# A two-block transformer in float32 on one core: logarithm tables loaded behind the last gate function, embedding products kept in PSUM, and the output projections in another order

## What is computed

```python
# first block, layers i = 0 and 1
        x = x + mixer(rms_norm(x))
        x = x + conv_ffn(rms_norm(x, ffn_norm[i]))
        gate = jax.nn.sigmoid(rms_norm(x, ple_norm[i]) @ ple_w_gate[i])
        x = x + gate * (p[i] @ ple_w_proj[i])

# second block, layers i = 0 and 1
        x = x + mixer(rms_norm(x))
        h = rms_norm(x)
        x = x + (silu(h @ w1) * (h @ w3)) @ w2
```

## Time and profile before

| | us |
|---|---|
| median of the runs | 1351.99 |
| lowest and highest of 3 | 1349.96, 1353.1 |
| profiled execution | 1347.64 |
| its span, first to last instruction | 1345.9 |
| TensorE busy in it | 1303.2 (97%) |
| GpSimd, ScalarE, VectorE busy | 1011.1, 677.4, 652.5 |
| share of the chain of waits on TensorE | 82% |

### The profile page before, as it was taken

The page is one execution under the profiler, slowest core; times in us unless marked ns, Lnnn a source line. Parts: engine busy times, 40 slices in busy tenths (PEclk is TensorE's granted clock), DMA queues, the critical chain, the costliest instruction groups (busy, mean ns, idle before and its releaser), DMA issues.

```text
span 1345.9 us, 27777 instructions
## 1 busy us (share of the span) xinstructions
PE 1303.2 (97%) x11032; PEld 1254.4 (93%) x11032; DVE 652.5 (48%) x1160; ACT 677.4 (50%) x934; POOL 1011.1 (75%) x793
## 2 busy tenths in 40 slices
PE   7989999999989999999999999999999999999999
PEld 6879999999989888999999878999999898999999
DVE  8994465555565748555566474211113545311112
ACT  7715544444666756444346565444435445533442
POOL 1226898888777649888878794988887665988885
PEclk9999999999999999999999999999999999999999
DMA  6313675555535335555554532555554432555530
GB/s 265 127 64 127 183 248 181 176 179 183 188 128 182 103 124 171 185 185 187 185 175 143 188 134 95 197 178 182 185 187 165 139 114 93 188 189 188 180 131 31
DMA packets 33879, 217.07 MB, mean 161 GB/s; under 512 B 3683, under 2 KB 7428, under 8 KB 8196
## 3 DMA queue, kind: packets, MB, share of 16 engines
q1 hardware_dynamic: 30096, 211.14, 44.5%
q10 hardware_dynamic: 3700, 4.75, 1.4%
HBM read 213.26 MB, written 2.62 MB: 160 GB/s over the span
## 4 chain that ended last, share of the span: by engine, by line
PE 82%; DVE 8%; ACT 4%; issue 2%; POOL 2%; DMA 1%; DVEq 0%; ACTq 0%; SPq 0%; POOLq 0%
PE up L1510 19%; PE up L1511 18%; PE up L1512 18%; PE acc L1510 7%; PE acc L1512 6%; PE acc L1511 6%; PE up L1630 1%; DVE opnd L913 1%; ACT w_hi L477 1%; POOL w_lo L393 1%; DVE s_work L1053 1%; PE side L1716 1%; DVE s_work L1062 1%; ACT opnd L613 1%; PE acc L2090 0%
## 5 line engine op out<-in xcount | busy, mean ns | idle before, releaser
L393 POOL TENSOR_TENSOR w_lo<-ring,w_hi 128x512 fp32r<-128x512 f32 x752 | 965.5, 1317 | 250.6 <-ACT w_hi L477 248.5
L1510 PE MATMUL up<-opnd,w_hi 128*128 128x256 f32 x2112 | 606.5, 287 | 10.5 <-POOL w_lo L393 4.2
L1511 PE MATMUL up<-opnd,w_lo 128*128 128x256 f32 x2112 | 597.4, 283 | 0.0
L1512 PE MATMUL up<-opnd,w_hi 128*128 128x256 f32 x2112 | 597.3, 283 | 0.0
L477 ACT ACTIVATE w_hi<-ring 128x2048 fp32r<-128x2048 f32 x190 | 362.6, 1909 | 258.7 <-PE up L1512 205.0
L1510 PEld LDWEIGHTS up<-opnd,w_hi 128*128 128x128 f32 x2112 | 404.7, 192 | 24.0 <-issue 16.6
L1511 PEld LDWEIGHTS up<-opnd,w_lo 128*128 128x128 f32 x2112 | 404.9, 192 | 1.2 <-issue 1.0
L1512 PEld LDWEIGHTS up<-opnd,w_hi 128*128 128x128 f32 x2112 | 404.8, 192 | 0.0
L1510 PE MATMUL acc<-opnd,w_hi 128*128 128x256 f32 x768 | 217.9, 284 | 2.6 <-DVE opnd L1154 2.6
L1511 PE MATMUL acc<-opnd,w_lo 128*128 128x256 f32 x768 | 217.3, 283 | 0.0
L1512 PE MATMUL acc<-opnd,w_hi 128*128 128x256 f32 x768 | 217.3, 283 | 0.0
(11 more groups left out here) (286 smaller groups left out, 1403.8 us busy)
## 6 DMA issues: line engine op xcount, KB each, us to landing
ring<-in_stream SPq DMA_DIRECT2D x197, 1024.0 KB, 4.8
bias_rows<-mix ACTq DMA_DIRECT2D x1, 1536.0 KB
mix<-in_s_b SPq DMA_DIRECT2D x1, 1024.0 KB, 5.5
x<-in_x SPq DMA_DIRECT2D x1, 1024.0 KB, 7.7
mix<-in_s_c SPq DMA_DIRECT2D x1, 1024.0 KB, 11.7
mix<-bias_rows ACTq DMA_DIRECT2D x1, 1024.0 KB, 5.4
out_x<-x SPq DMA_DIRECT2D x8, 128.0 KB, 1.7
mix<-in_p ACTq DMA_DIRECT2D x2, 256.0 KB, 4.4
```

Source lines behind the costliest of these rows:

```text
L393: ins = nc.gpsimd.tensor_tensor(w_l[:, cols], ring[:, r, cols], w_h[:, cols].bitcast(f32), ALU.subtract)
L1510: MM(o, l_hi, r_hi, start=start, stop=False, skip_group_check=True)
L1511: MM(o, l_lo, r_hi, start=False, stop=False, skip_group_check=True)
L1512: return MM(o, l_hi, r_lo, start=False, stop=stop, skip_group_check=True)
```

## The change

It moves the table load from the head of `rms` to other places (`root_tables`): behind the last Sigmoid of the GLU, behind the last slot of feed-forward 0, 1 and 2, and behind the last Sigmoid of each embedding stage. In front of ffn1, ffn2 and ffn3, where Ln and Exp are in the tables already, it leaves the load out. It keeps the embedding products in PSUM: VectorE writes gate times product over the product in `acc` and adds from there. It takes the stick-breaking results straight from PSUM for both operand parts. It does slot 1 of the projections wo and out before slot 0 (WO_DONE, OUT_DONE), and the feed-forward stages behind them take the input tiles in the order 2, 3, 0, 1, 4 to 7; the copy of the next stage's first weights stands ahead of all operand tiles (lead=4). Slots 2 and 3 of the projection out use the banks `acc[:, 0]` and `acc[:, 1]`, slot 3 has its split weights in `mix`, and two input tiles of slot 2 come before the last tiles of slots 0 and 1. The last down slot of each feed-forward stage does four output tiles with the first h tile before it waits for the second.

```diff
+        last_hi = {START["out"] + 3: mix_r[:, 0:2048],
...
+        last_lo = {START["out"] + 3: mix_r[:, 2048:4096],
...
+                elif s == START["out"] + 3:
+                    act.wait_ge(sem("z_ps"), 8)
+                elif s in (START["ffn1"], START["ffn3"]):
+                    act.wait_ge(sem("mm_done"), s - 3)
...
             def rms(tokens=False, folded=True):
 
-                nc.scalar.preload_act_table_set("natural_log_exp_and_others")
                 c.wait("ssq")
...
                 if m == KT - 1:
+                    root_tables()
                     high_parts_to(s + 3)
                 operand_tile("ffn0", m)
...
                 if end:
+                    root_tables()
                     high_parts_to(S + 34)
...
                     c.up(A(f_c[:, 2 + e], f_u[:, 2 + e, 2:258], ACT.Sigmoid), "gated")
+                    if e:
+                        root_tables()
                     operand_tile(end, 6 + e)
...
-            residual("ffn1", START["wo"], lead=3)
+            residual("ffn1", START["wo"], lead=4, groups=WO_DONE)
...
-                    high_parts_to(S + min(t // 2, 12) + 2)
+                    high_parts_to(S + min(t // 2, 13) + 2)
...
-                    from_psum("stick", p, aux[p % 2][:, 0:T], k_out)
-            residual("ffn3", START["out"])
+                    c.up(A(hi("stick")[:, p], aux[p % 2][:, 0:T], ACT.Copy), "hi_ready")
+            residual("ffn3", START["out"], lead=4, groups=OUT_DONE)
...
-                    step(V.tensor_tensor(f_c[:, b:b + 2], f_c[:, b:b + 2],
-                                         acc[:, g].rearrange("p (a t) -> p a t", a=2), ALU.mult))
+                    prod = acc[:, g].rearrange("p (a t) -> p a t", a=2)
+                    step(V.tensor_tensor(prod, f_c[:, b:b + 2], prod, ALU.mult))
...
-                        c.up_and_wait(V.tensor_tensor(x[:, m], x[:, m], f_c[:, b + e], ALU.add), "x_ready")
+                        c.up_and_wait(V.tensor_tensor(x[:, m], x[:, m], prod[:, e], ALU.add), "x_ready")
...
+            def last_down_slot(s, ops):
+
+                slot_ready(s)
+                c.wait("h_ready")
+                for m in range(KT // 2):
+                    down_tile(s, ops, m, 0, False, True)
+                c.wait("h_ready")
+                for m in range(KT):
+                    for k in range(1 if m < KT // 2 else 0, 2):
+                        ins = down_tile(s, ops, m, k, False, True)
+                    if m % 2 and m < KT - 1:
+                        c.up(ins, "acc_bank")
+                c.up(ins, "mm_done")
...
-                    28: [(0, rest), (1, rest)], 29: [(2, rest), (3, rest)]}
+                    28: [(1, rest), (0, rest)], 29: [(2, rest), (3, rest)]}
...
-                    28: [(0, [6]), (1, [6])], 29: [(0, [7]), (1, [7])]}
+                    27: [(2, range(2))], 28: [(1, [6, 7]), (0, [6, 7])], 29: [(2, range(2, KT)), (3, range(KT))]}
...
-            for g in range(2, 4):
-                up_slot("stick", out + g)
-            ffn(3, "ffn3")
+            ffn(3, "ffn3", OUT_DONE)
```

More of the change, by code:

```diff
@@ L1547, in up_slot @@
                 w_h, w_l = weights_hi(s), weights_lo(s)
-                for k in range(KT):
+                for j, k in enumerate(order):
                     if fresh:
@@ L1758, in _, with ffn @@
                          "bias_ps")
-            def ffn(l, name):
+            def ffn(l, name, groups=range(4)):
                 S = START[f"ffn{l}"]
+                order = [m for g in groups for m in (2 * g, 2 * g + 1)]
                 assert used[0] == BANK[f"ffn{l}"]
-                up_slot(name, S, fresh=True, sums=True)
+                up_slot(name, S, fresh=True, sums=True, order=order)
                 up_slot(name, S + 1, fold=True)
@@ L1784, in ffn @@
                 used[0] += 3 * 4
-                down(S + 32, 0, last=True, each=True)
+                last_down_slot(S + 32, 0)
             def ple(l):
```

93 lines of the change are left out of this document (48 added, 45 removed).

## The result

| | before | change |
|---|---|---|
| median of 5 runs each | 1351.17 | 1338.0 |
| lowest to highest | 1349.87 to 1353.1 | 1337.6 to 1343.82 |
| profiled execution | 1347.64 | 1337.60 |
| its span | 1345.9 | 1335.8 |

The ratio is 0.9900 with a 95% interval of 0.9882 to 0.9918: 13.5 us less (11 to 16). The two profiled executions differ by 10.0 us.

A forecast was written before the change was run, and what follows sets the result against it. TensorE, busy 1303.2 of 1345.9 us, bounds the kernel, so only its waits can shrink: 0.65 + 0.27 + 3.6 + 0.2 - 0.4 + 3.5 = 7.8 us, median 1344.2, range 1339.5 to 1349.0.

The forecast's parts named there:

- GLU: Border from GLU to first feed-forward: moving the table load removes TensorE's wait, gain 0.65 us, between 0 and 0.65.
- Ends of feed-forward 0 and 1: Last down slots: the second h tile's wait mostly reappears a slot later at the adds; gains 0.13 and 0.14 us.
- Embedding stages: Both embedding stages: faster PSUM adds (1.1 us) and no load before the sum (0.70); gain 1.8 each, 3.6 together.
- Output projection to feed-forward 1: After differential attention: GpSimd's wait shrinks, but the chain to the all-sums matmul takes most; gain 0.2 us, -1.2 to +1.6.
- wait of 1.5 to 2 for the copy of the sum: Sign of being right at differential attention's output projection: this TensorE wait, in us, replaces the one for GpSimd.
- End of feed-forward 2: Border to the last attention: load delays the first low tile, sum's wait goes; net -0.4 us, -1.5 to +0.24.
- Last projection: Last output projection to feed-forward 3: slots 2 and 3 ready in time, hole closes; gain 3.5 us, 3.0 to 3.7.
- A rule against it: The Trainium skill's 1380 ns drain on top of each 1283 ns table load, 2.66 us per load; the rows show none.
- the second rival: Moved loads hold ScalarE another 1.3 us, costing 4.2 at ends of feed-forward 0 to 2: 1348.4 us; chance 0.13.
- The median: Whole kernel: the median's 4.35 us above the profiled execution carries over, so profiled 1339.8 gives median 1344.2.
- The first rival: Stalls at the borders go entirely: gain 13.1 us, with 11 or more about 1340; chance 0.10.
- The clock rival: TensorE's granted clock falls more often once the resting gaps close, making the kernel slower, median 1356 us; chance 0.03.

The follow-up runs named there:

- f4: The kernel before, unchanged, profiled a fourth time; one run, 1351.52 us.
- e3: The changed kernel with the embedding's products written to SBUF again and added from there; median 1342.16 us, ratio 0.9911 to before.
- e5: The changed kernel with each feed-forward stage's last down slot waiting for both h tiles first, as before; median 1339.73 us, ratio 0.9920 to before.
- e6: The changed kernel with differential attention's output projection in the old order, slot 0 first, next weights copied one slot later; median 1341.81 us, ratio 0.9931 to before.
- e2: The changed kernel with every table load back at the head of the norm (21 loads); median 1345.10 us, ratio 0.9938 to before.
- e4: The changed kernel with the loads from the ends of feed-forward 0, 1 and 2 moved to where ScalarE is idle; median 1338.87 us, ratio 0.9893 to before.
- f1: The changed kernel again, unchanged, on another batch beside the kernel before; median 1343.38 us, ratio 0.9927 to before.
- f2: e4 with the absolute value of the stick-breaking logits made by ScalarE and not VectorE; median 1336.22 us, ratio 0.9875 to before.

## Why the prediction was right and wrong

- **What bounds the kernel** held: TensorE's busy time only went from 1303.2 to 1301.9, and the other 8.8 of the 10.1 are its waits at borders.
- **GLU**, 0.65: measured 0.81. DMA and tile 7 did as said; the wait went wholly, and the gap around it was a little wider than the idle time that the row names. In f4 the wait was not there to begin with and the gain would be 0.1: the lower bound of 0 was the right one, for another reason than the one given.
- **Ends of feed-forward 0 and 1**, 0.13 and 0.14: the mechanism was right. The wait went from the h tile to the adds in the next down slot (0.59). The lead grew by 1.13 and 1.07 there and at tiles 6 and 7 together; less e3's 0.94 that leaves 0.19 and 0.13. e5 has 0.4 for both and the last attention.
- **Embedding stages**, 1.8 each: 1.9 each, 0.94 for the products by e3 and 0.97 and 0.96 for the sum by the lead. I had 1.1 and 0.70. Tile 6's wait went wholly; tile 7's, which I had shortened too, stayed at 0.98. (Of the eight adds of a stage six took 0.88 before and two 0.75, so VectorE saved 3.4 and not up to 3.7.)
- **Output projection to feed-forward 1**, 0.2: this is the term of the sum that failed, with 1.68 measured. The step "Without the load it is 5.87, so the matmul comes at 511.0 + 5.87 = 516.9" took the DMA of p inside the chain as it stood in the trace. The adds came where forecast: 507.04 in the change, plus the lead of 3.10, is 510.14, and I had 510.2. But the chain behind them was 4.48 (507.90 to 512.38) and not 5.87, and TensorE did not wait for it at all:

```profile
507.04 0.86 DVE L1235 TENSOR_TENSOR x<-x,acc 128x256 f32<-128x256 f32 x2
...
510.51 0.73 ACT L676 ACTIVATE opnd<-mix 128x256 fp32r<-128x256 f32 x2 [1.51 <-DMA mix<-in_p]
...
512.38 0.38 PE L1536 MATMUL side<-rstd,par 128*128 128x256 f32 x1
```

Before, the DMA's landing was awaited for 3.19 (L668, at 514.59), here for 1.51. Its times from issue to landing, the two DMAs of p (behind the GLU and here), before and in the change:

```profile
DMA to landing us min/median/max: 4.2/4.4/4.6
```

```profile
DMA to landing us min/median/max: 2.5/3.4/4.2
```

The reason is in the DMA share by single us. Before, p is issued at 510.0 together with a 1 MB transfer of the ring:

```profile
510.00:511.00 1.00, 1.00 (x11) 1.00 (x10) 0.58 (x1) 1.00 (x3) 1.00 (x2) 1.00 0.88 188
511.00:512.00 1.00, 1.00 (x13) 0.87 (x12) 1.00 (x2) 0.41 (x2) 1.00 (x2) 1.00 0.96 401
512.00:513.00 1.00, 1.00 (x13) 0.59 (x13) 1.00 (x1) 0.00 (x0) 1.00 (x2) 1.00 0.96 401
```

In the change (rows below) it is issued at 507.9, when the ring's transfer is over, since GpSimd had given the ring buffer back sooner: it starts on the next stage's first slot at 497.30, with the lead of 3.10 at 500.4, and not at 503.29 as before. SP, which waits for that, issues the transfer at 503.10 and not at 509.05.

```profile
507.00:508.00 1.00, 1.00 (x13) 0.46 (x12) 0.86 (x3) 0.75 (x3) 1.00 (x1) 1.00 0.22 90
508.00:509.00 1.00, 1.00 (x10) 1.00 (x10) 0.77 (x2) 1.00 (x3) 1.00 (x2) 1.00 0.05 14
509.00:510.00 1.00, 1.00 (x10) 0.95 (x8) 0.97 (x1) 0.00 (x1) 0.69 (x1) 1.00 0.86 240
```

e6 puts the old order back and has the 4.6 again, and in e2, which keeps the new order but not the moved load, p takes 2.6 and TensorE waits 0.48. So the wait of 1.5 to 2 for the copy of the sum, which the forecast named as a sign of being right, did not come. That TensorE would have waited with a landing of 4.6 is worked out from the rows, not tested. I had followed the weights that come free earlier to ScalarE and GpSimd, but not on to SP's queue.

- **End of feed-forward 2**, -0.4: measured -0.18. The load did push the first low tile by one operation of GpSimd, and e4 gets it back.
- **Last projection**, 3.5: measured 3.32 and 0.15 in front of it.
- **A rule against it**: the moved load behind the first embedding stage's last Sigmoid starts 0.02 behind its end (379.40 + 0.40) and takes 1.28; behind it ScalarE waits for VectorE. The moved load at the end of feed-forward 0 has work on both sides, 0.02 away and 0.01 away:

```profile
339.49 1.91 ACT L487 ACTIVATE w_hi<-ring 128x2048 fp32r<-128x2048 f32 x1
341.42 1.28 ACT L503 ACT_TABLE_LOAD   x1
342.71 0.51 ACT L619 ACTIVATE opnd<-x,par 128x256 fp32r<-128x256 f32 x1
```

Nothing drains, and the second rival fell.

- **The median**: the step "The median of the runs is 1351.99, 4.35 us above it, so I carry the difference over to the median" failed in the first comparison, and it is this step that put the time out of the range: the measured 10.0 between the profiled executions and the 4.35 would have given 1342.0, within it. The change's median is 0.4 above its profiled execution. Four of its first five runs lie at 1337.6 to 1338.2. The profiled execution of before was free of both kinds of events and had an early start (109.95 at the GLU, against 110.47, 111.89 and 111.18 in its other three profiles), so it lay 2.2 to 5.5 below its own other runs. That those runs hold the events is likely from the later profiles, but they were not profiled. In f1's batch two of the change's six runs are at 1339.96, the profiled one of them with VectorE's wait, and four at 1343.1 to 1343.7, of which no profile exists; their median of 1343.4 is close to the forecast's 1344.2, by events that the forecast did not have. In the first comparison the step is 3.9 us of the miss of 6.2, the sum of the borders 2.3 (10.1 for 7.8). The first rival (1340, stalls go entirely) comes nearest in time, but not in mechanism: the waits for the adds and for tile 7 stayed, as I had it.
- **The clock rival** (holes are rest, and without them the grant falls) went the other way in every profile: from the GLU to the last matmul the grant fell behind holes, and in none of the kernels with fewer of them did it fall elsewhere. The change closes two of the places. That this makes such events rarer is argued, not shown: four profiles of before and two of the change give no rate, and the hole at the start of the GLU, behind which four of the seven falls lie, is in both kernels.

## What to carry to other kernels

Follow a buffer that comes free earlier through every engine up to the queue that refills it: the transfer that it triggers earlier decides how long an unrelated small DMA takes. Price a two-SBUF-operand instruction of VectorE beside a train of GpSimd operations at both of its values, since which one it takes changes from run to run, and give such an instruction on a critical chain to ScalarE, as f2 does, or take one operand from PSUM, as the embedding stages do. Look at where in a program the profiled execution's time lies among the runs before you carry its offset over: it can be an execution without the events that the others have.

## What the runs showed of the hardware that I had not expected

- One instruction of VectorE with both operands in SBUF (128 x 768 float32) took 1.97 us or 4.50 in the same kernel (the change's first profile and f1); in the long case it ended 0.82 behind the last of GpSimd's queued operations.
- From the start of the GLU on, TensorE's grant fell to 0.50 behind 7 of 28 waits of 1.97 to 2.40 us and behind none of the shorter ones, of up to 1.6; a fall cost 1.2 to 1.6 us.
- A DMA of 256 KB took 2.5 us from issue to landing where the DMA engines had little else in its first microsecond (a share of 0.05) and 4.6 beside a 1 MB transfer (0.96).
- A table load took 1.28 us in all places, 18 times in the change, and at the places shown here no idle time of its own lay around it. What it cost TensorE depended on what stood behind it on ScalarE: up to 3.0 us in all for the ones moved or left out.
